# Even mixer of a two-block transformer: the scores of four forgetting heads in one TensorE group instead of two

## Chip, cores, metric

The kernel runs on one core of a Trainium2 chip. The metric is the device time of one execution in microseconds (us); a kernel's time is the median of its runs.

## What is computed

Two transformer blocks with 256 rows of 1024 columns run one after the other, each two layers deep. The change lies in the second block, in the even mixer of its first layer, which holds eight forgetting heads of width 64 beside four differential heads:

```python
def forgetting_attention(q, k, v, cum_logf):
    ...
    for qs in range(0, seq, Q_BLOCK):
        qe = qs + Q_BLOCK
        s = jnp.einsum('bqhd,bkhd->bhqk', q[:, qs:qe], k[:, :qe], preferred_element_type=jnp.float32) * scale
        s = s + cum_logf[:, :, qs:qe, None] - cum_logf[:, :, None, :qe]
        causal = jnp.arange(qs, qe)[:, None] >= jnp.arange(qe)[None, :]
        p = jax.nn.softmax(jnp.where(causal, s, -jnp.inf), axis=-1).astype(v.dtype)
        outs.append(jnp.einsum('bhqk,bkhd->bqhd', p, v[:, :qe]))
    return jnp.concatenate(outs, axis=1)

def even_mixer(h, w_in, ...):
    a_q, a_k, a_v, a_f, b_q, b_k, b_v = split_cols(h @ w_in, EVEN_SIZES)
    aq = rms_norm(a_q.reshape(bsz, seq, A_HEADS, HEAD_DIM), qk_gains[0])
    ak = rms_norm(a_k.reshape(bsz, seq, A_HEADS, HEAD_DIM), qk_gains[1])
    ...
    a_out = forgetting_attention(aq, ak, av, cum_logf).reshape(bsz, seq, A_WIDTH)
    ...
    b_out = differential_attention(bq, bk, bv, lam)
    b_out = (rms_norm(b_out, subln_gain) * (1.0 - lambda_init)).reshape(bsz, seq, B_WIDTH)
    return jnp.concatenate([a_out, b_out], axis=-1) @ w_out
```

After the mixer comes attention to a memory of 256 rows, whose keys and values (`mem_n @ w_kv`) do not depend on the mixer.

## The kernel before

**Large matmuls.** All weights stream from HBM. A unit of weights is 1024 columns wide in SBUF. ScalarE rounds it to `WH` (L1358), VectorE takes the rest as `WL` (L1647), and TensorE multiplies three times: `WH` and `WL` by the high part of the rows, `WH` by their low part (L1081, L1082, L1083). The three passes for 128 rows of the contraction and one of the two row tiles are called a step of large matmuls. Five units of `WH` and `WL` are held; ScalarE converts the next when TensorE has used up the oldest (`w_used`). A projection of 512 columns (a chunk) fills two of four large banks of PSUM, M0 and M1 or M2 and M3, one for each row tile.

**Small steps between them.** Four other banks, AUX0 to AUX3, serve all small products: turns (transposes of results that become rows for the next projection), scores, transposes of probabilities, products with the values. A small step takes the bank that the planner expects to be free first. TensorE waits at it until the bank's last user has been read out (`aux_out`).

**A forgetting head** goes through these steps. The scores of two heads (64 rows each, in the two halves of TensorE's rows) are one step on TensorE: L1242 and L1244 for the even head, L1243 and L1245 for the odd one, each head into its own AUX bank. VectorE adds the decay and the causal mask and takes the row maximum (L1929, L1930). ScalarE takes the exponentials with their sums into a buffer TMP, and with that the bank is free (L1563, L1564). VectorE divides by the sums (L1956 to L1961). TensorE transposes the three blocks of 128x128 (L1252) into another AUX bank, and ScalarE copies them to `PT` (L1585). After four heads TensorE multiplies them by the values (L1279, L1281), and ScalarE and VectorE take the high and low part of the result (L1529, L1703).

**The neighbours.** Around these steps the stage ends the differential heads: their outputs (L1263 to L1265) and two turns of their normalised result `BO` (L1124), read out by ScalarE (L1421) and VectorE (L1680). The large matmuls that run meanwhile are the memory's keys (`MTh`, `MTl`), two chunks, then the mixer's output projection (`XA0h`, `XA0l`). ScalarE evicts each chunk of keys with the sums of squares of its heads (L1401, L1405), and VectorE reduces them (L1865).

**The order.** `Plan` builds every step with a place `at`, counted in contraction steps of a 512-column chunk, one for both row tiles. TensorE takes the steps in the order of `at`. ScalarE and VectorE each take them in the order of `at` plus the step's own `late` plus a constant for the step's kind:

```python
act, dve = (sorted(steps, key=lambda s: (s.at + s.late + LATER.get(s.kind, (0.0, 0.0))[i], s.rank, s.seq)) for i in range(2))
```

For scores that constant is 2.2 on ScalarE and 0.9 on VectorE. The places of the forgetting heads come from the table `PLACES`: in `heads`, the scores of heads 2p and 2p+1 stand at `at + hg_s[p]`, where `at` is the end of the chunk of values; `hg_late[p]` is added for the odd head; normalisation, transposes and the products with the values stand at `hg_p`, `hg_pt` and `hg_o` behind the place of their own pair. Within an engine nothing is reordered at run time.

Of the kernel before, what the change touches and what calls it, by code (L numbers as in the profile page):

```python
# [32 lines left out]
    "df_late": (1.5, 0.6, -0.6, -0.1), "df_p": (3.1, 3.4, 3.4, 3.4), "df_pt": (5.9, 6.8, 6.2, 6.8), "df_o": (7.4, 9, 10.5, 8.3),  # L33
    "bo": (28, 28.5, 29.2, 30.1, 34.4, 36.7), "hg_s": (1.3, 6.6, 11.6, 16.3), "hg_late": (1.3, 1.3, 1.9, 2.5),
    "hg_p": (3, 5.4, 4.2, 5.4, 4.2, 5.4, 4.2, 6.6), "hg_pt": (5.6, 6.8, 5.6, 6.2, 5, 7.4, 6.5, 7.4), "hg_o": (7.6, 8.2),
    "od_s": (0.9, 6, 9.8, 15.5), "od_late": (0, 1.3, -1.2, 1.3), "od_p": (3, 5.4, 4.2, 4.2, 1.7, 5.4, 4.8, 6),
    "od_pt": (5.6, 9.3, 5.3, 7.5, 5.3, 6.5, 6.5, 7.7), "od_o": (9.6, 11.9), "odd": (25.7, 17.5, 0, 14.2, 0, 14.8, -7.2),
# [2366 lines left out]
```

## Time and profile before

| | us |
|---|---|
| median of 3 runs | 1864.65 (1864.58 to 1866.2) |
| profiled execution | 1865.1 |
| its span | 1862.7 |
| TensorE busy in the span | 1857.9 |
| VectorE, ScalarE busy | 1310.3, 1119.3 |
| the changed stage in the span | about 1018 to 1063 |

Times in the rows below are microseconds from the start of the span. TensorE is called PE there, its weight loads PEld, VectorE DVE, ScalarE ACT, GpSimd POOL and SyncE SP. In the chain of work a row's time is the step by which the end of the work moves on; in the timeline it is the instruction's own duration, which overlaps the next.

### The profile page before, as it was taken

Reading aid. Unit: us, or ns where it says so; the run is one execution under the profiler, and the core shown is the slowest. Engines: PE = TensorE matmul, PEld = TensorE weight load, DVE = VectorE, ACT = ScalarE, POOL = GpSimd, SP = SyncE. Lnnn points to the kernel's source line nnn. Section 1 sums busy time; section 2 is a strip of 40 time slices with the busy share of each in tenths; the row PEclk is TensorE's granted clock in tenths of the full one; section 3 lists DMA queues with packets and bytes.
Section 4 is the critical chain, followed back from the end, with each engine's and each line's share of the span. In section 5 each row is a group of like instructions: output and inputs, shape, how many; then the busy total and the mean of one; then the engine's idle time right before and its main releaser. Section 6 shows DMA issues by size and latency. Waiting matters only on the chain.

```text
span 1862.7 us, 25413 instructions
## 1 busy us (share of the span) xinstructions
PE 1857.9 (100%) x9293; PEld 1623.7 (87%) x9293; DVE 1310.3 (70%) x1949; ACT 1119.3 (60%) x1678; POOL 369.0 (20%) x606
## 2 busy tenths in 40 slices
PE   9999999999999999999999999999999999999999
PEld 8888988888889888888888889888888888899888
DVE  6776776667777776666577886776666578977664
ACT  6776655557766655555468785654555467765553
POOL 2101233111001431122103001531122111102320
PEclk9999999999999999999999999999999999999999
DMA  9767789878578997798765567997798788758984
GB/s 316 236 186 229 222 258 299 260 233 253 166 221 242 292 287 232 219 272 255 238 180 191 174 191 204 281 274 237 225 255 252 227 265 242 216 157 232 255 258 138
DMA packets 289803, 436.43 MB, mean 234 GB/s; under 512 B 25548, under 2 KB 170416, under 8 KB 289424
## 3 DMA queue, kind: packets, MB, share of 16 engines
q1 hardware_dynamic: 260384, 352.41, 61.9%
q0 software_dynamic: 28832, 82.07, 16.3%
q8 instruction: 74, 1.21, 0.3%
q14 instruction: 49, 0.40, 0.1%
q10 hardware_dynamic: 464, 0.34, 0.1%
HBM read 396.43 MB, written 38.29 MB: 233 GB/s over the span
## 4 chain that ended last, share of the span: by engine, by line
PE 99%; DMA 0%; DVE 0%; SPq 0%; ACT 0%; issue 0%; ACTq 0%
PE M L1081 31%; PE M L1083 31%; PE M L1082 31%; PE AUX L1124 1%; PE AUX L1138 0%; PE AUX L1252 0%; DMA RAW<-in_w_in 0%; PE AUX L1244 0%; PE AUX L1242 0%; PE AUX L1279 0%; PE AUX L1167 0%; PE AUX L1295 0%; PE AUX L1323 0%; PE AUX L1296 0%; PE AUX L1297 0%; PE AUX L1324 0%
## 5 line engine op out<-in xcount | busy, mean ns | idle before, releaser
L1647 DVE TENSOR_TENSOR WL<-RAW,WH 128x1024 fp32r<-128x1024 f32 (+1 forms) x669 | 810.8, 1217 | 383.5 <-ACT WH L1358 380.9
L1358 ACT ACTIVATE WH<-RAW 128x1024 fp32r<-128x1024 f32 (+1 forms) x670 | 705.0, 1055 | 518.8 <-PE M L1083 469.7
L1081 PE MATMUL M<-WH,Bh 128*128 128x512 f32 (+1 forms) x1820 | 691.3, 380 | 0.6 <-ACT TMP L1401 0.3
L1082 PE MATMUL M<-WL,Bh 128*128 128x512 f32 (+1 forms) x1820 | 683.1, 375 | 0.0
L1083 PE MATMUL M<-WH,Bl 128*128 128x512 f32 (+1 forms) x1820 | 683.1, 375 | 0.0
L1081 PEld LDWEIGHTS M<-WH,Bh 128*128 128x128 f32 x1820 | 344.2, 189 | 50.6 <-issue 4.2
L1083 PEld LDWEIGHTS M<-WH,Bl 128*128 128x128 f32 x1820 | 344.2, 189 | 47.1
L1082 PEld LDWEIGHTS M<-WL,Bh 128*128 128x128 f32 x1820 | 344.4, 189 | 44.7
L1396 ACT ACTIVATE AS<-M,KEEP 128x256 f32<-128x256 f32 x132 | 55.3, 470 | 80.3 <-PE M L1083 78.7
L1081 PE MATMUL M<-WH,MTh 128*128 128x512 f32 x128 | 51.0, 398 | 0.0
L1082 PE MATMUL M<-WL,MTh 128*128 128x512 f32 x128 | 48.5, 379 | 0.0
L1083 PE MATMUL M<-WH,MTl 128*128 128x512 f32 x128 | 48.5, 379 | 0.0
L2085 POOL DMA_DIRECT2D squares<-QT x4 | 3.0, 762 | 171.2 <-DVE QT L1772 171.2
L2098 POOL DMA_DIRECT2D HB0t<-squares x48 | 26.3, 555 | 50.0 <-DMA squares<-HB0b 45.7
L2098 POOL DMA_DIRECT2D HB1t<-squares x48 | 26.4, 556 | 47.0 <-DMA squares<-HB1b 30.0
L1745 DVE SCALAR_TENSOR_TENSOR X<-M,X 128x512 f32<-128x512 f32 (+1 forms) x54 | 30.5, 607 | 6.1 <-PE M L1083 6.1
L2098 POOL DMA_DIRECT2D HC0t<-squares x48 | 26.3, 554 | 43.1 <-DMA squares<-HC0b 42.2
L2078 POOL TENSOR_TENSOR KEEP<-SM,KEEP 128x2 f32<-128x2 f32 x15 | 13.3, 885 | 108.1 <-DVE SM L1723 98.6
L2098 POOL DMA_DIRECT2D HD0t<-squares x48 | 26.4, 557 | 41.2 <-DMA squares<-HD0b 41.1
L1082 PE MATMUL M<-WL,LA1h 128*128 128x512 f32 (+1 forms) x94 | 34.4, 366 | 0.0
L1083 PE MATMUL M<-WH,LA1l 128*128 128x512 f32 (+1 forms) x94 | 34.4, 366 | 0.0
L1081 PE MATMUL M<-WH,LA1h 128*128 128x512 f32 (+1 forms) x94 | 34.4, 366 | 0.0
(534 smaller groups left out, 2886.9 us busy)
## 6 DMA issues: line engine op xcount, KB each, us to landing
RAW<-in_ffn_w_in SPq DMA_DIRECT2D x352, 256.0 KB, 4.2
RAW<-in_w_in SPq DMA_DIRECT2D x103, 512.0 KB, 4.8
RAW<-in_w_gate_up SPq DMA_DIRECT2D x176, 256.0 KB, 4.4
RAW<-in_ffn_w_out SPq DMA_DIRECT2D x88, 512.0 KB, 4.6
RAW<-in_w_down SPq DMA_DIRECT2D x44, 512.0 KB, 4.9
RAW<-in_x_w_kv SPq DMA_DIRECT2D x32, 512.0 KB, 4.6
RAW<-in_even_w_in SPq DMA_DIRECT2D x24, 512.0 KB, 4.5
RAW<-in_odd_w_in SPq DMA_DIRECT2D x24, 512.0 KB, 5.4
```

The costliest lines, as they stand in the source:

```text
L1081: e.matmul(out, s.hi, wh, start=s.at0, stop=False)
L1082: e.matmul(out, s.hi, wl, start=False, stop=False)
L1083: i = e.matmul(out, s.lo, wh, start=False, stop=s.final)
L1124: tr = e.transpose(aux[:, i * P:(i + 1) * P], x, ident)
L1358: e.activation(hi, raw, ACT.Copy).then_inc(k.w_hi, 1)
L1396: e.activation(s.silu[t], banks[t][:, 0, :], ACT.Silu, scale=r[t]).then_inc(k.silu_made, 1)
L1647: e.tensor_tensor(lo, raw, hi.bitcast(F32), ALU.subtract).then_inc(k.w_lo, 1)
L1745: e.scalar_tensor_tensor(out=x, in0=banks[t], scalar=s.scale, in1=x, op0=ALU.mult, op1=ALU.add).then_inc(k.m_out[c.banks[t]], 1)
L2078: e.tensor_tensor(s.r, s.v, p.MHALF, ALU.pow).then_inc(k.r_made, 1)
L2085: e.dma_start(p.parked[x.slot, 0:4 * P * 32 * x.m].rearrange("(c p e) -> p c e", c=n, p=P), x.squares.rearrange("p (c e) -> p c e", c=n)). ...
L2098: e.dma_start(x.rows[32 * c:32 * c + 32, :].rearrange("p (q e) -> p q e", q=q), p.parked[x.slot, c * n:(c + 1) * n].rearrange("(q j e) -> ...
```

## The change

One row of numbers. The scores of heads 0 and 1 move from 1.3 to 6.6, where heads 2 and 3 stand; those of heads 4 and 5 move from 11.6 to 16.3, where heads 6 and 7 stand. The odd heads' delay on ScalarE and VectorE falls from 1.3 to 2.5 down to 0 for the first pair of a group and 0.6 for the second. Normalisations and transposes move with their scores, since they are placed relative to them; the products with the values stand where they did.

```diff
-    "bo": (28, 28.5, 29.2, 30.1, 34.4, 36.7), "hg_s": (1.3, 6.6, 11.6, 16.3), "hg_late": (1.3, 1.3, 1.9, 2.5),
+    "bo": (28, 28.5, 29.2, 30.1, 34.4, 36.7), "hg_s": (6.6, 6.6, 16.3, 16.3), "hg_late": (0, 0.6, 0, 0.6),
```

**TensorE, the first group of scores.** `KA` and `QA` are the heads' keys and queries, `M0` to `M3` the large banks, `CC` the identity for transposes. Before, heads 2 and 3 stand alone, with a transpose of head 0 behind them:

```order
L1083 MATMUL M1<-WH,MTl 128x512
L1242 MATMUL AUX1<-KA,QA 128x128
L1243 MATMUL AUX2<-KA,QA 128x128
L1244 MATMUL AUX1<-KA,QA 128x256
L1245 MATMUL AUX2<-KA,QA 128x256
L1252 MATMUL AUX3<-CC,TMP1 128x128 x3
L1081 MATMUL M0<-WH,MTh 128x512
```

With the change:

```order
L1083 MATMUL M1<-WH,MTl 128x512
L1242 MATMUL AUX0<-KA,QA 128x128
L1243 MATMUL AUX2<-KA,QA 128x128
L1244 MATMUL AUX0<-KA,QA 128x256
L1245 MATMUL AUX2<-KA,QA 128x256
L1242 MATMUL AUX1<-KA,QA 128x128
L1243 MATMUL AUX3<-KA,QA 128x128
L1244 MATMUL AUX1<-KA,QA 128x256
L1245 MATMUL AUX3<-KA,QA 128x256
L1081 MATMUL M0<-WH,MTh 128x512
```

Heads 0 and 1 came some ten steps earlier and now stand in the same group: four heads hold all four AUX banks.

**ScalarE, the exponentials behind the first chunk of keys.** Before (the exponentials of heads 0 and 1 stand further up, outside this piece):

```order
L1585 ACTIVATE PT0<-AUX0 128x384
L1401 ACTIVATE TMP1<-M0,KEEP 128x512
L1405 ACTIVATE AS<-TMP1 128x512
L1401 ACTIVATE TMP4<-M1,KEEP 128x512
L1405 ACTIVATE AS<-TMP4 128x512
L1563 ACTIVATE TMP0,SM<-AUX1,SM 128x128
L1564 ACTIVATE TMP0,SM<-AUX1,SM 128x256
L1358 ACTIVATE WH<-RAW 128x1024
L1563 ACTIVATE TMP3,SM<-AUX2,SM 128x128
L1564 ACTIVATE TMP3,SM<-AUX2,SM 128x256
L1421 ACTIVATE XA0h<-AUX3 128x512
```

With the change (behind the last row follow a conversion L1358, the turn's L1421 from AUX0, another L1358 and the copies L1585):

```order
L1401 ACTIVATE TMP4<-M0,KEEP 128x512
L1405 ACTIVATE AS<-TMP4 128x512
L1401 ACTIVATE TMP5<-M1,KEEP 128x512
L1405 ACTIVATE AS<-TMP5 128x512
L1563 ACTIVATE TMP0,SM<-AUX0,SM 128x128
L1564 ACTIVATE TMP0,SM<-AUX0,SM 128x256
L1563 ACTIVATE TMP1,SM<-AUX2,SM 128x128
L1564 ACTIVATE TMP1,SM<-AUX2,SM 128x256
L1563 ACTIVATE TMP2,SM<-AUX1,SM 128x128
L1564 ACTIVATE TMP2,SM<-AUX1,SM 128x256
L1563 ACTIVATE TMP3,SM<-AUX3,SM 128x128
L1564 ACTIVATE TMP3,SM<-AUX3,SM 128x256
```

All four heads' exponentials now stand behind the eviction of the chunk of keys in M0 and M1, heads 0 to 3 in TMP0 to TMP3. On TensorE the first turn, which wrote AUX3 before, now writes AUX0.

**TensorE's transposes and VectorE's normalisations of the first group, with the change.** TensorE, from the first transposes on (the first turn, L1124 into AUX0, stands four steps of large matmuls ahead):

```order
L1252 MATMUL AUX1<-CC,TMP0 128x128 x3
L1252 MATMUL AUX2<-CC,TMP2 128x128 x3
L1081 MATMUL M3<-WH,MTh 128x512
L1082 MATMUL M3<-WL,MTh 128x512
L1083 MATMUL M3<-WH,MTl 128x512
L1124 MATMUL AUX3<-CC,BO 128x128 x4
L1252 MATMUL AUX0<-CC,TMP3 128x128 x3
```

VectorE, from head 2's normalisation on:

```order
L1956 RECIPROCAL SM<-SM 128x2
L1960 TENSOR_SCALAR TMP2<-TMP2,SM 128x128
L1961 TENSOR_SCALAR TMP2<-TMP2,SM 128x256
L1647 TENSOR_TENSOR WL<-RAW,WH 128x1024
L1680 TENSOR_TENSOR XA0l<-AUX0,XA0h 128x512
L1956 RECIPROCAL SM<-SM 128x2
L1960 TENSOR_SCALAR TMP1<-TMP1,SM 128x128
L1961 TENSOR_SCALAR TMP1<-TMP1,SM 128x256
L1956 RECIPROCAL SM<-SM 128x2
L1960 TENSOR_SCALAR TMP3<-TMP3,SM 128x128
L1961 TENSOR_SCALAR TMP3<-TMP3,SM 128x256
```

Head 0 is normalised before this piece, then head 2, and heads 1 and 3 only after a weight conversion and the turn's low part. TensorE transposes heads 0, 2, 3 and 1 in this order; before, the four transposes lay between the large matmuls one by one.

## Rows read from the trace of the kernel before

**Rows 1.** The page: span, engines' busy time, granted clock in 40 slices

```profile
span 1862.7 us, 25413 instructions
PE 1857.9 (100%) x9293; PEld 1623.7 (87%) x9293; DVE 1310.3 (70%) x1949; ACT 1119.3 (60%) x1678; POOL 369.0 (20%) x606
...
PEclk9999999999999999999999999999999999999999
```

**Rows 2.** TensorE's waits over the span: us in total, times, longest us

```profile
PE M L1031 <- DVE WARM L1621: 1.1, 1, 1.1
...
PE M L1081 <- ACT TMP L1401: 0.3, 1, 0.3
```

**Rows 3.** The chain of work, 1030 to 1042: start us, us, what

```profile
1030.94 0.48 PE AUX L1252 x3
...
1037.37 0.22 PE M L1081
1037.58 0.22 PE M L1082
1037.80 0.21 PE M L1083
...
1038.66 0.30 PE AUX L1242
...
1038.97 0.10 PE AUX L1242
...
1039.52 0.41 PE M L1081
...
1040.36 0.33 PE AUX L1252 x3
...
1041.34 0.44 PE AUX L1124 x4
```

**Rows 4.** ScalarE's timeline, 1032 to 1038: start us, us, instruction [idle before <-releaser]

```profile
1032.81 1.06 ACT L1358 ACTIVATE WH<-RAW 128x1024 fp32r<-128x1024 f32 x1 [0.87 <-PE M L1083]
1033.78 0.48 ACT L1585 ACTIVATE PT<-AUX 128x384 f32<-128x384 f32 x1
1034.14 0.68 ACT L1401 ACTIVATE TMP<-M,KEEP 128x512 f32<-128x512 f32 x1
...
1036.63 0.35 ACT L1563 ACTIVATE TMP<-AUX,SM 128x128 f32<-128x128 f32 x1
...
1037.42 1.05 ACT L1358 ACTIVATE WH<-RAW 128x1024 fp32r<-128x1024 f32 x1
```

**Rows 5.** TensorE's timeline: the first matmul of the second chunk of keys

```profile
1032.55 0.38 PE L1081 MATMUL M<-WH,MTh 128*128 128x512 f32 x1
```

**Rows 6.** VectorE's timeline, 1033 to 1041

```profile
1033.57 0.30 DVE L1929 CUSTOM_DVE_ANT_0 AUX<-AUX,NB 128x128 f32<-128x128 f32 x1
...
1034.79 1.23 DVE L1647 TENSOR_TENSOR WL<-RAW,WH 128x1024 fp32r<-128x1024 f32 x1
1035.93 1.52 DVE L1865 TENSOR_REDUCE SM<-AS 128x2 f32<-128x512 f32 x2
...
1037.56 0.17 DVE L1956 RECIPROCAL SM<-SM 128x2 f32<-128x2 f32 x1
...
1037.96 0.35 DVE L1961 TENSOR_SCALAR TMP<-TMP,SM 128x256 f32<-128x256 f32 x1
1038.51 1.23 DVE L1647 TENSOR_TENSOR WL<-RAW,WH 128x1024 fp32r<-128x1024 f32 x1 [0.19 <-ACT WH L1358]
1039.80 0.69 DVE L1680 TENSOR_TENSOR XA0l<-AUX,XA0h 128x512 fp32r<-128x512 f32 x1
1040.40 0.15 DVE L1956 RECIPROCAL SM<-SM 128x2 f32<-128x2 f32 x1
```

**Rows 7.** ScalarE's copy of the eighth head, and the product with the values that waits for it

```profile
1060.41 0.49 ACT L1585 ACTIVATE PT<-AUX 128x384 f32<-128x384 f32 x1 [1.14 <-PE AUX L1252]
...
1061.04 0.65 PE L1279 MATMUL AUX<-PT,VA 128*64 128x256 f32 x4
```

## Prediction

> **What bounds the kernel now.** Read the page first: TensorE is busy for the whole span and its granted clock stands at full speed in every slice [rows 1]. Then TensorE's waits: the longest after the opening is 0.3 us, and nothing near the changed place is in the list [rows 2]. So the order of TensorE's queue is the time: whatever is taken out of that queue is gained in full, and whatever makes it stand is lost in full, because no wait later on is long enough to take it back. The third view is the chain of work through the forgetting heads [rows 3]. It shows at what intervals TensorE ends its work, and so what a group of scores costs beyond its own columns. The last is the timelines of ScalarE and VectorE there [rows 4, 6]: both have work in hand and small gaps, and they follow TensorE. What matters is how far behind it they are when TensorE needs one of their results.
>
> **What the change takes out.** The scores of a pair of heads are eight short passes. A pair standing alone pays on the way in: its first pass takes 0.30 us, the same pass of the second half 0.10 us, so 0.20 us is extra. It pays on the way out: the large matmul behind it takes 0.41 us instead of 0.22, 0.19 us extra [rows 3]. One of the four pairs is followed by transposes, which take 0.48 instead of 0.33 us, 0.15 us extra [rows 3]. Before: 4 x 0.20 + 3 x 0.19 + 0.15 = 1.52 us. After: two groups of two pairs, 2 x (0.20 + 0.19) = 0.78 us. **Saving 0.74 us.** The trace has no two pairs back to back. Inside a pair the step from one head's half to the next costs nothing [rows 3], which is the nearest row, so I take the full saving; the other end is that the second pair pays as if it stood alone, a saving of nothing. Nothing else is removed: row maxima, exponentials, normalisations, transposes and copies are as many as before, no transfer is added, and the queues of POOL and SP are not touched.
>
> **What it adds: two waits behind the first group.** Write T for the moment when TensorE finishes the chunk of memory keys in banks M0 and M1. That chunk ends two steps of large matmuls after the group. Behind T TensorE's new order is: five steps of large matmuls (three passes of 0.22, 0.22 and 0.21 us, 0.65 us each [rows 3]), so 3.25 us, and then the first turn of the differential result, which now writes AUX0. AUX0 holds the scores of head 0 and comes free when ScalarE has taken head 0's exponentials. Before, this turn wrote AUX3, long free.
>
> ScalarE's new order puts all four heads' exponentials behind the eviction of that same chunk. From T, by its rows: the conversion of the next weights starts 0.26 us after the next chunk's first matmul (1032.81 against 1032.55 [rows 4, 5]); it is followed 0.97 us later; the eviction with its squares takes 1034.14 to 1036.63, 2.49 us; one head's exponentials take 1036.63 to 1037.42, 0.79 us [rows 4]. From the end of a ScalarE result to TensorE's start on it are 0.14 us (1060.90 to 1061.04 [rows 7]). Sum 0.26 + 0.97 + 2.49 + 0.79 + 0.14 = 4.65 us. **First wait 4.65 - 3.25 = 1.40 us.** Before, heads 0 and 1 had their exponentials ahead of this eviction, and nothing on TensorE hung on heads 2 and 3 so soon.
>
> The second wait is at the transposes of head 3, third of the four transposes in TensorE's new order. They need head 3's normalised rows, and VectorE normalises in the order 0, 2, 1, 3. It puts a weight conversion and the low part of the turn ahead of heads 1 and 3. That conversion needs the ScalarE conversion that now stands behind the four exponentials. From T: 0.26 + 0.97 + 2.49, four heads 4 x 0.79 = 3.16, the ScalarE conversion 1.05 [rows 4], hand-over 0.04 (1038.47 to 1038.51 [rows 4, 6]), VectorE's conversion 1.14 (1034.79 to 1035.93), the turn's low part 0.60 (1039.80 to 1040.40), two normalisations of 0.75 (1037.56 to the end of L1961 at 1038.31 [rows 6]) and 0.14 to TensorE: 11.35 us. TensorE's own work from T to there: nine steps of matmuls 5.85, two turns 0.88 (0.44 each), two heads' transposes 0.66, one more step 0.65: 8.04 us. **Both waits together 11.35 - 8.04 = 3.31 us**, of which 1.91 us is the second. What is queued behind TensorE in both waits is everything, since its queue is in order.
>
> The reductions of the squares (1.52 us at 1035.93 [rows 6]) stand ahead of head 2 on VectorE, but run under ScalarE's exponentials and conversion. The row maxima are not late: two heads take 1033.57 to 1034.79, 1.22 us, four 2.44 us [rows 6]; with a conversion of 1.14 us ahead they end about 2.3 us behind T, and ScalarE asks for the first at 0.26 + 0.97 + 2.49 = 3.72 us. All four banks are free when the group starts: the last user of AUX3, the differential output, is now 8 steps of matmuls, 5.2 us, ahead of it.
>
> Bounds of the 3.31 us: if heads 1 and 3 did not have to stand behind VectorE's conversion it would be 1.14 us less, 2.2 us; if ScalarE's conversion meets a weight buffer that TensorE, standing still, has not yet released, half a microsecond more, 3.8 us. I take 3.3, as each term has its row.
>
> **The second group** has ten steps of matmuls, 6.5 us, before its first transposes, and no turn writes one of its banks. But the transposes of its last two heads now stand back to back, one step of matmuls ahead of the product with the values; there the chain shows TensorE with hardly any slack now (the copy ends at 1060.90, the product starts at 1061.04 [rows 7]). I add 0.1 us, between 0 and 0.4.
>
> **Sum:** -0.74 + 3.31 + 0.10 = +2.67 us. The profiled execution took 1865.1 us (span 1862.7 us) and would become 1867.8; it is 0.45 us above the median of the three runs, 1864.65, so the forecast against that median is **1867.3 us**. With the bounds, +1.5 to +4.0: 1866.1 to 1868.7. About 0.2%, 3.7 us, is what a measurement of this kernel can tell from no change, so this is no measurable change, on the slow side.
>
> The rows say that a group over all four banks leaves the turn no free one. Of the Trainium skill, Perfetto Trace Analysis, section Matmuls, says that independent groups should rotate through the banks, so that one is evacuated under the next one's matmuls; that speaks against this change. By it alone the whole 4.65 us to the first free bank would be lost, 3.25 us more than here; the rows put five steps of matmuls over it, so I do not follow it that far.
>
> **The rivals.** (a) The banks come free in time: ScalarE reaches the exponentials earlier than its order lets me see, and the saving stands alone, -0.74 + 0.10: 1864.0 us. For it: ScalarE has gaps of up to 0.87 us there [rows 4]. Against: the gap ends with the release of the very chunk it must evict. Chance 0.10. (b) Only the first wait comes, VectorE being ahead: -0.74 + 0.10 + 1.40, 1865.4 us. Chance 0.10. (c) Slower: the second group stalls as the first does, at the transposes of its last head. By the same rows its last normalisation ends about 0.4 us before TensorE asks for it, so it decides if ScalarE, which evicts the next keys first, begins the exponentials 0.4 us later than I have it. The price is at most that of the second wait, 1.91 us: 1869.2 us. Chance 0.10. (d) The pairs do not share their way in and out: +0.74, 1868.0 us. Chance 0.03. (e) The clock falls. It is at full speed throughout, also around the 1.1 us wait at the start [rows 1, 2]; should it go to half from the first wait to the product with the values, some 5.2 us of work would take as much again: 1872.5 us. TensorE: Matmul & The Clock Gate of the Trainium skill (A second HAM failure mode) tells of such a fall where the engine idles often between groups as it cycles through banks. Two waits in one place are not often. Chance 0.03. The forecast keeps 0.64.
>
> **The numbers.** The range leaves out (a) and (e), 0.13, and takes in (b), (c) and (d): 1865.0 to 1869.3 us. Slower by over 0.2% means above 1868.4: (c), (e) and the upper end of the forecast, 0.14. Faster by over 0.2% needs 3.7 us, and there is no such amount to save: 0.02. No change by that measure: 0.84.
>
> **What would show it.** In the changed profile TensorE's waits should list the turn L1124 with about 1.4 us, waiting for ScalarE's L1564, and the transposes L1252 with about 1.9 us, waiting for VectorE's L1961; the chain should show 0.30 and 0.41 us at two groups instead of four. The first product with the values should come about 1.9 us later than before, the second 2.7 us. No wait at L1124 or L1252 would make me wrong, and so would a third one of over a microsecond in the second group.

## The result and the profile after

The changed kernel takes **1867.44 us** (median of 22 runs, 1866.91 to 1868.7). The kernel before, run beside it, takes 1865.01 us (22 runs, 1864.39 to 1867.08). The ratio is 1.0013 with a 95% interval of 1.0007 to 1.0019: slower by 2.4 us. The interval does not hold 1, so the loss is there, but it lies within the 0.2% that counts as no change here. The profiled execution took 1866.96 us, its span is 1865.2 us.

The page of the changed kernel, the lines that answer to [rows 1]:

```profile
span 1865.2 us, 25412 instructions
PE 1857.2 (100%) x9293; PEld 1623.9 (87%) x9293; DVE 1309.8 (70%) x1949; ACT 1119.1 (60%) x1678; POOL 369.4 (20%) x606
...
PEclk9999999999999999999999999999999999999999
```

The clock is still full in every slice, the same instructions run on TensorE, and its busy time is even 0.7 us less than in [rows 1]. The span is 2.5 us longer all the same, so TensorE must stand somewhere. TensorE's waits over the span of the changed kernel (us in total, times, longest us) say where:

```profile
PE AUX L1252 <- DVE TMP L1961: 1.5, 1, 1.5
PE AUX L1124 <- ACT TMP L1564: 1.3, 1, 1.3
```

Both lines are new against [rows 2], and no others of that size are. TensorE's timeline of the changed kernel shows where they stand, and that the group itself has become cheaper:

```profile
1028.95 0.37 PE L1242 MATMUL AUX<-KA,QA 64*128 64x128 f32 x1
...
1029.16 0.27 PE L1242 MATMUL AUX<-KA,QA 64*128 64x128 f32 x1
...
1029.70 0.27 PE L1242 MATMUL AUX<-KA,QA 64*128 64x128 f32 x1
1029.81 0.27 PE L1242 MATMUL AUX<-KA,QA 64*128 64x128 f32 x1
...
1036.60 0.63 PE L1124 MATMUL AUX<-CC,BO 128*128 128x128 f32 x4 [1.34 <-ACT TMP L1564]
...
1043.05 0.55 PE L1252 MATMUL AUX<-CC,TMP 128*128 128x128 f32 x3 [1.49 <-DVE TMP L1961]
...
1063.57 0.65 PE L1279 MATMUL AUX<-PT,VA 128*64 128x256 f32 x4
```

From the first pass to the second the first pair takes 0.21 us, the second pair 0.11 us: the second pair pays no way in. The first wait ends at the first turn, the second at the third of the four transposes. The first product with the values starts at 1045.80, 1.82 us later than in the kernel before (1043.98), the second at 1063.57, 2.53 us behind [rows 7].

The executions do not all begin the stage at the same moment: its first output of a differential head (L1263) starts between 1018.12 and 1019.08 us in the profiles below, for reasons further up in the span that are not followed here. So I compare kernels by **the distance** from that L1263 to the second product. It is 42.91 us before (1018.13 to 1061.04) and 45.45 us with the change (1018.12 to 1063.57): +2.54 us, all of the difference in the span.

The chain of work through the second wait, as the changed kernel's chain has it (start us, us, what):

```profile
1035.65 0.35 ACT TMP L1563 x2
...
1038.42 0.46 ACT TMP L1564 x2
1038.87 0.96 ACT WH L1358
1039.83 0.02 issue
1039.86 1.23 DVE WL L1647
1041.08 0.60 DVE XA0l L1680
...
1042.74 0.27 DVE TMP L1961
1043.01 0.04 issue
1043.05 0.55 PE AUX L1252 x3
```

It runs through four exponentials, one ScalarE conversion, one VectorE conversion, the turn's low part and two normalisations. That is the order that the prediction counted up.

### The profile page after: what moved, and what is told of

It reads as the page before. It is cut to its first block, busy times and chain, and to the rows that moved or that the text cites. A ratio compares the mean times of both kernels' runs of the same rounds, so it can differ in the third digit from the quotient of the medians.

```text
span 1865.2 us, 25412 instructions
## 1 busy us (share of the span) xinstructions
PE 1857.2 (100%) x9293; PEld 1623.9 (87%) x9293; DVE 1309.8 (70%) x1949; ACT 1119.1 (60%) x1678; POOL 369.4 (20%) x606
## 3 DMA queue, kind: packets, MB, share of 16 engines
q8 instruction: 74, 1.21, 0.3%
## 4 chain that ended last, share of the span: by engine, by line
PE 98%; ACT 0%; DVE 0%; DMA 0%; SPq 0%; issue 0%; ACTq 0%
PE M L1081 31%; PE M L1083 31%; PE M L1082 31%; PE AUX L1124 1%; PE AUX L1138 0%; PE AUX L1252 0%; DMA RAW<-in_w_in 0%; PE AUX L1244 0%; DVE WL L1647 0%; PE AUX L1242 0%; PE AUX L1279 0%; PE AUX L1167 0%; PE AUX L1295 0%; PE AUX L1323 0%; PE AUX L1297 0%
## 5 line engine op out<-in xcount | busy, mean ns | idle before, releaser
L1358 ACT ACTIVATE WH<-RAW 128x1024 fp32r<-128x1024 f32 (+1 forms) x670 | 704.7, 1055 | 518.2 <-PE M L1083 471.2
L2098 POOL DMA_DIRECT2D HC1t<-squares x48 | 26.3, 556 | 39.4 <-DMA squares<-HC1b 39.4
```

Of the source, the lines that this page charges most:

```text
L1358: e.activation(hi, raw, ACT.Copy).then_inc(k.w_hi, 1)
L2098: e.dma_start(x.rows[32 * c:32 * c + 32, :].rearrange("p (q e) -> p q e", q=q), p.parked[x.slot, c * n:(c + 1) * n].rearrange("(q j e) -> ...
```

## The experiments

The theory: what costs time is the order on ScalarE and VectorE, and the bank that the turn holds; the group of four itself is cheaper. The rival: four heads at once are a longer chain, and cost it wherever their steps stand. Each experiment is judged by the distance against the kernel before (+2.54 us is the change's), taken from one profiled execution of each kernel; the edit of experiment 2, profiled again as experiment 8, gave the same distance to 0.01 us. Every diff below is against the changed kernel.

| experiment | TensorE's waits in the stage, us, in order | distance against before, us | runs | time, us |
|---|---|---|---|---|
| the change | L1124 1.34, L1252 1.49 | +2.54 | 22 | 1867.44 |
| 1 first group only | L1124 1.35, L1252 0.62 and 1.23 | +3.64 | 1 | 1868.1 |
| 2, 8 second group only | L1252 0.48; 0.48 | +0.36; +0.35 | 1; 11 | 1866.33; 1865.65 |
| 3 normalisations ahead | L1124 1.35, L1252 1.21 | +2.25 | 1 | 1866.93 |
| 4, 9 turns later | L1252 1.17 and 1.91; 1.16 and 1.91 | +4.44; +4.21 | 1; 10 | 1869.12; 1869.11 |
| 5 exponentials ahead | L1252 1.26 and 1.42 | +2.42 | 1 | 1866.97 |
| 7 exponentials and normalisations ahead | L1252 1.44 | +0.93 | 1 | 1865.58 |
| 6 all three | none | -0.46 | 11 | 1864.48 |

### 1. Only the first group

```diff
-    "hg_s": (6.6, 6.6, 16.3, 16.3), "hg_late": (0, 0.6, 0, 0.6),
+    "hg_s": (6.6, 6.6, 11.6, 16.3), "hg_late": (0, 0.6, 1.9, 2.5),
```

> Only heads 0 to 3 stand in one group; heads 4 to 7 as before. If the loss lies behind the first group (theory): TensorE still waits about 1.3 us at L1124 and 1.5 us at L1252, and the second product with the values starts at about 1063.9 (1063.57 with the change, plus 0.37 for the way in and out that the second group no longer shares, less up to 0.1). If it lay in holding four banks as such, half of it would go: waits of about 1.4 us in all, about 1062.4.

1868.1 us. TensorE's waits in this kernel:

```profile
PE AUX L1252 <- DVE XA0l L1680: 1.9, 2, 1.2
PE AUX L1124 <- ACT TMP L1564: 1.4, 1, 1.4
```

The wait for the exponentials is the change's. Behind it the transposes wait twice, and for L1680, VectorE's low part of a turn: here they go to a bank that a turn still holds. With heads 4 and 5 left at 11.6, their scores stand on TensorE between these steps, hold two of the four banks, and take one more way in and out. So the first group is what costs, and half of the change costs 1.10 us more (3.64 - 2.54) than all of it. The theory had the first wait right. The second it had as one of 1.5 us, where two came, 1.85 us together and for L1680, and the second product came at 1064.69 instead of 1063.9. The rival's 1.4 us of waits in all does not hold either. Of the 1.10 us, 0.37 is listed waiting (3.20 against 2.83) and 0.37 is what the expectation reckons for the way in and out; the rest is not accounted for.

### 2 and 8. Only the second group

```diff
-    "hg_s": (6.6, 6.6, 16.3, 16.3), "hg_late": (0, 0.6, 0, 0.6),
+    "hg_s": (1.3, 6.6, 16.3, 16.3), "hg_late": (1.3, 1.3, 0, 0.6),
```

> Only heads 4 to 7 stand in one group. Theory: no wait of TensorE above 0.3 us beside those of the kernel before; the second product with the values at about 1060.8 (1061.04 before, less 0.37 for one way in and out, plus 0.1). If a group of four costs by itself (rival), a wait of 1 us or more at its transposes and about 1062.

1866.33 us, but this execution began the stage at 1019.06 us, 0.93 us late. By the distance the edit costs 0.36 us, where the theory had a gain of 0.24 us (1060.8 against 1061.04) and no wait over 0.3 us: a miss. A wait of 0.48 us came. It was therefore run again with more runs:

> Only heads 2 and 3 moved to the later place (three groups of TensorE in the layer instead of four or two), as in the first look at this edit, with more runs, to see whether the 0.93 us that the profile was late ahead of the place, and the 0.5 us wait for L1961, come again. Theory (half the change has half the saving and a small wait): second product 0 to 0.5 us later than in the kernel before, reckoned from the first L1263 of the layer, median within 0.6 us of before, ratio 0.9998 to 1.0003. Rival (any group moved costs the whole chain): second product 2 us later, ratio 1.0010 or more.

(The heads that this edit moves are 4 and 5; the text on record misnames them.) Median 1865.65 us against 1865.05, ratio 1.0003 (0.9994 to 1.0012). This profile began only 0.26 us late, and its distance is +0.35 us. The wait came again, in TensorE's timeline:

```profile
1041.46 0.55 PE L1252 MATMUL AUX<-CC,TMP 128*128 128x128 f32 x3 [0.48 <-DVE TMP L1961]
```

The wait is not in the second group. It stands at head 3's transposes in the first, where the scores of heads 4 and 5 stood before (1038.66 to 1039.52 in [rows 3]). Taking them away took cover from VectorE's normalisation: VectorE ends it 23.02 us behind the first L1263 in this kernel (1041.41) as in the kernel before (1041.15), but TensorE is there 0.9 us earlier. The small price, which the second expectation had, holds; the rival's 2 us does not.

### 3. The normalisations ahead of the reductions and the conversion

```diff
-    "hg_p": (3, 5.4, 4.2, 5.4, 4.2, 5.4, 4.2, 6.6),
+    "hg_p": (3.2, 3.3, 3.4, 3.5, 4.2, 5.4, 4.2, 6.6),
```

> VectorE normalises heads 0, 1, 2 ahead of the reductions of the squares and head 3 right behind them, all ahead of the weight conversion. If the second wait comes from heads 1 and 3 standing behind the conversion (as the prediction had it in its lower bound), it shrinks by about 1.1 us: L1252 waits 0.4 us, second product at about 1062.4. If VectorE's whole work on that stretch sets it (rival), the bank AUX0 stays shut by the turn's low part L1680 instead, only VectorE's idle 0.57 us goes, L1252 waits about 0.9 us for L1680, and the product starts at about 1063.0. The first wait stays at 1.3 us by both.

1866.93 us, distance +2.25. Head 3's normalised rows are there at 1041.16, but TensorE starts its transposes at 1043.03. TensorE's and VectorE's timelines of this kernel:

```profile
1043.03 0.52 PE L1252 MATMUL AUX<-CC,TMP 128*128 128x128 f32 x3 [1.21 <-DVE XA0l L1680]
```

```profile
1040.81 0.35 DVE L1961 TENSOR_SCALAR TMP<-TMP,SM 128x256 f32<-128x256 f32 x1
1041.07 1.22 DVE L1647 TENSOR_TENSOR WL<-RAW,WH 128x1024 fp32r<-128x1024 f32 x1
1042.20 0.68 DVE L1680 TENSOR_TENSOR XA0l<-AUX,XA0h 128x512 fp32r<-128x512 f32 x1
```

The wait shrank by 0.28 us, not by the 1.14 us of the conversion, and has another releaser. So the theory's 0.4 us fails; the rival named the right releaser, but had 0.9 us for the 1.21. Head 3's transposes go to AUX0, where the first turn stands until L1680 has read it, and L1680 stands behind the same conversion. The second wait has two holders, one behind the other.

### 4 and 9. The turns behind head 3's transposes

```diff
-    "bo": (28, 28.5, 29.2, 30.1, 34.4, 36.7),
+    "bo": (28, 28.5, 29.2, 30.1, 37.2, 38.3),
```

> Both turns of the differential result move behind the transposes of head 3, so that no turn writes a bank of the group before its exponentials. If the two waits are two causes (rival), the 1.3 us at L1124 go and the rest stays: second product at about 1062.1. If one chain from the chunk's end over ScalarE and VectorE to head 3 sets the sum (theory), the waits move to the transposes L1252 of heads 2 and 3 and still come to about 3.4 us: second product at 1063.6 to 1063.9.

1869.12 us, distance +4.44. No wait is left at L1124; the transposes wait 1.17 and 1.91 us, 3.08 together instead of 2.83. Taking the first wait away gains nothing, since the same chain on ScalarE and VectorE is met one step later. So the rival fails, and the theory's waits came, 0.3 us short of the 3.4 expected, but the second product came at 1065.72 instead of 1063.6 to 1063.9. Some 1.6 us of the +4.44 are not in the waits, and the windows of this kernel show what they are (us, busy of PE, PEld, DVE, ACT, POOL, then the granted clock, the DMA share and GB/s):

```profile
1042.00:1043.00 1.00, 0.30 (x2) 0.30 (x3) 0.96 (x4) 0.00 (x0) 0.00 (x0) 0.90 0.13 43
1043.00:1044.00 1.00, 1.00 (x5) 0.91 (x4) 0.78 (x1) 0.41 (x1) 0.00 (x0) 0.50 0.94 346
1044.00:1045.00 1.00, 1.00 (x4) 0.71 (x4) 0.00 (x0) 0.08 (x1) 0.00 (x0) 0.50 0.47 166
1045.00:1046.00 1.00, 1.00 (x8) 1.00 (x6) 0.00 (x0) 0.00 (x0) 0.00 (x0) 0.50 0.68 203
1046.00:1047.00 1.00, 1.00 (x6) 0.92 (x5) 0.00 (x0) 0.63 (x2) 0.00 (x0) 0.89 0.78 299
```

The clock falls to half at the end of the second wait. To see whether that belongs to the order or to the one execution, it was run again:

> The change with TensorE's turns for the norm behind head 3's transposes, as in the first look at this edit, to see whether the granted clock falls again behind the two waits that stand close together. Theory (the order of the waits makes the clock fall): a stretch of two us behind the second wait again with a granted clock of 0.5 to 0.7, and 1868.5 to 1869.5 us, ratio 1.0018 to 1.0026. Rival (chance of that one execution): granted clock 1.00 in every stretch, 1866.5 to 1867.5 us, ratio 1.0008 to 1.0015.

1869.11 us (10 runs), ratio 1.0021 (1.0012 to 1.003), as the theory had it. The fall came again, at the same place in the order, this time within the wait, which ends at 1043.41:

```profile
1042.00:1043.00 1.00, 0.00 (x0) 0.00 (x0) 0.93 (x6) 0.48 (x2) 0.00 (x0) 0.99 0.00 0
1043.00:1044.00 1.00, 0.59 (x4) 0.60 (x4) 1.00 (x3) 0.00 (x0) 0.00 (x0) 0.50 0.75 90
```

It did not come every time. In 7 of the 10 runs the mean clock of the span was 0.999, and their median is 1869.59 us; in three it was 1.000, and these are the three fastest, 1867.25 to 1867.98 us, where the rival had 1866.5 to 1867.5. TensorE's timeline gives the price. The eight starts from these transposes to the second large matmul behind the next ones

```profile
1043.41 0.90 PE L1252 MATMUL AUX<-CC,TMP 128*128 128x128 f32 x3 [1.91 <-DVE TMP L1961]
...
1046.86 0.38 PE L1082 MATMUL M<-WL,MTh 128*128 128x512 f32 x1
```

take 3.45 us (1043.41 to 1046.86). The steps between them at full clock are 0.30 + 0.30 + 0.22 + 0.22 + 0.43 + 0.25 + 0.30 = 2.02 us, the first four from other places of this kernel, the last three from the kernel before, where a turn and transposes follow each other too. The fall costs 1.43 us here, and by the same reckoning 1.67 us in the first execution (1042.70 to 1046.39, 3.69 us). With it the distances add up: the change's, the longer waits and the fall are 2.54 + 0.25 + 1.67 = 4.46 us in experiment 4 (measured 4.44) and 2.54 + 0.24 + 1.43 = 4.21 us in experiment 9 (measured 4.21).

### 5. The exponentials ahead of the eviction of the keys

```diff
-                s.late = PLACES[f"{which}_late"][hp] * hh
+                s.late = PLACES[f"{which}_late"][hp] * hh - (1.2 if which == "hg" and hp < 2 else 0)
```

> All four heads' scores at the later place as in the change, but the exponentials and row maxima of heads 0 to 3 are put ahead of the evictions of the four chunks on ScalarE and VectorE. Theory (VectorE runs its instructions in order, and the reductions of the chunks' squares, now waiting for the later evictions, and the squares' conversion still stand between the four normalisations): the wait at L1124 goes, L1252 waits 1.6 to 2.0 for head 2 and 1.4 to 1.7 for head 3, 3.0 to 3.7 together, and the second product with values comes 2.2 to 3.0 us later than in the kernel before, no earlier than in the change. Rival (the eviction ahead of the exponentials alone makes the wait): both waits go, the second product comes 0.5 to 0.8 us earlier than before.

The term counts on both engines, so VectorE's row maxima move up with the exponentials. 1866.97 us, distance +2.42. TensorE's waits:

```profile
PE AUX L1252 <- DVE TMP L1961: 2.7, 2, 1.4
```

The wait at L1124 is gone, as both expected. The exponentials of head 3 end at 1035.84 instead of 1038.88, three microseconds earlier, and the kernel gains 0.12 us: the normalisations of heads 2, 1 and 3 still stand on VectorE behind the reductions of the squares, which end 0.6 us later than in the change (1039.05 against 1038.43), and those of heads 1 and 3 behind the conversion and L1680 as well. The theory gave 3.0 to 3.7 us for the two waits, and no gain on the change; it is 2.68, a little less, with that gain of 0.12. The rival, that the exponentials alone make the wait, falls.

### 7. Exponentials and normalisations ahead, the turns left

This is experiment 5 with 1.4 for 1.2, and with the first four numbers of `hg_p` at (1.3, 1.4, 1.5, 1.6).

> All four heads' scores at the later place; exponentials and normalisations of heads 0 to 3 ahead of the evictions and the reductions, as in the experiment with three edits, but TensorE's turns for the norm left where the change has them, so that the second turn's bank is held until VectorE's low parts of it (L1680), which stand behind the reductions and a conversion. Theory (the bank is a wait of its own): no wait at L1124, and L1252 ahead of the first product waits 0.7 to 1.4 for L1680; second product with values 0.3 to 1.0 us later than in the kernel before, reckoned from the first L1263 of the layer. Rival (with exponentials and normalisations early the bank does not matter): no wait over 0.3 us, second product 0.4 to 0.7 us earlier than before.

1865.58 us, distance +0.93. One wait is left, in TensorE's timeline, and VectorE's timeline (first the end of head 3's normalisation) shows that head 3 had been ready for 4.4 us:

```profile
1041.67 0.52 PE L1252 MATMUL AUX<-CC,TMP 128*128 128x128 f32 x3 [1.44 <-DVE XA0l L1680]
```

```profile
1036.92 0.35 DVE L1961 TENSOR_SCALAR TMP<-TMP,SM 128x256 f32<-128x256 f32 x1
...
1040.84 0.68 DVE L1680 TENSOR_TENSOR XA0l<-AUX,XA0h 128x512 fp32r<-128x512 f32 x1
```

So the bank is a holder by itself, worth 1.44 us, a touch more than the 0.7 to 1.4 expected.

### 6. All three

Experiment 7 with the turns at 37.2 and 38.3, as in experiment 4.

> All four heads' scores at the later place as in the change, with exponentials and all four normalisations ahead of the evictions and the reductions on their engines, and TensorE's turns for the norm behind the transposes of head 3. Theory (order on ScalarE, VectorE and the bank held by the turn together make the wait; the group itself is cheaper): no wait over 0.5 us at L1124 or L1252 before the first product, second product 0.4 to 0.8 us earlier than in the kernel before, 1864.2 to 1864.6 us, ratio 0.9995 to 0.9998. Rival (one group of four heads costs in itself, by its longer chain of four row maxima and exponentials ahead of any product): waits of 1 us or more stay at the transposes of heads 2 and 3, second product 0.5 to 2 us later than before, 1865.5 to 1867 us.

Median 1864.48 us (11 runs) against 1865.10 (15 runs), ratio 0.9998 (0.9989 to 1.0007). TensorE's waits over the whole span:

```profile
PE M L1031 <- DVE WARM L1621: 1.1, 1, 1.1
PE M L1081 <- ACT TMP L1401: 0.3, 1, 0.3
PE M L1081 <- DVE Bl L1674: 0.2, 1, 0.2
```

None is left in the stage, and the distance is 42.45 us, 0.46 less than before, near the low end of what the theory expected. The rival falls: four heads at once cost nothing when the work that follows them is not late and no turn holds their bank. Of the 0.74 us that the prediction had as saving, 0.27 is lost in one step of TensorE:

```profile
1040.30 0.60 PE L1124 MATMUL AUX<-CC,BO 128*128 128x128 f32 x4
1041.00 0.52 PE L1252 MATMUL AUX<-CC,TMP 128*128 128x128 f32 x3
```

From the turn to the transposes are 0.70 us, against 0.43 in the kernel before. What holds them is not in the list of waits, but ScalarE's timeline has a likely holder, the first of four copies of transposes:

```profile
1040.39 1.66 ACT L1585 ACTIVATE PT<-AUX 128x384 f32<-128x384 f32 x4
```

By the plan of this kernel these transposes, head 1's, write AUX0, which head 0's hold until that first copy. The copies take 0.48 us each, so it ends at 1040.87, 0.13 us ahead of the transposes, about the hand-over of 0.14 in [rows 7]. No experiment moved the copy. The kernel beats the change (1867.44). Against the kernel before it is 0.6 us lower by the medians, and its interval holds 1, so a gain over that one is not shown by the times.

## Why the prediction was right

Forecast 1867.3 us, measured 1867.44; forecast +2.67 us, measured +2.43 by the medians and +2.54 by the distance. Point by point, each by the steps from one start on TensorE to the next in the two timelines:

- **What bounds it.** The order of TensorE's queue is the time: the spans of the profiled executions follow their distances to within 0.3 us (leaving aside experiments 2 and 9, which began 0.9 us late), so no wait was made up for later.
- **The saving, forecast 0.74 us.** All steps but those at the turns and products came out 0.65 us shorter. The groups themselves give the whole 0.74, since the chain of the changed kernel has the way in, 0.30 us, only at 1029.02 and 1050.11 and the way out, 0.41 us, only at 1030.53 and 1051.62; the first steps behind the two waits are 0.08 us longer together (0.38 for 0.35 and 0.30 for 0.25). The second pair of a group shares the way in and out, so rival (d) falls.
- **The first wait, forecast 1.40 us.** The profile lists 1.34. The step from the last large matmul to the turn, with that of the second turn, grew from 0.44 to 1.93 us, 1.49 us. T, the end of the chunk in M0 and M1, is 1031.86 and the turn starts at 1036.60: 4.74 us, against 4.65 added up from rows.
- **The second wait, forecast 1.91 us.** Listed 1.49; the step from the turn to the transposes grew from 0.43 to 2.09 us, 1.66 us. From T to its end are 11.19 us, forecast 11.35. Both together 3.15 us, forecast 3.31: the term was 0.16 us too large. ScalarE's and VectorE's other steps came out within 0.04 us of their rows; the excess lies in the two normalisations (1.40 us, counted as 1.50) and the hand-over to TensorE (0.05, counted as 0.14). Experiments 5 and 7 show its parts, ScalarE's order, VectorE's order and the bank.
- **The second group, forecast 0.10 us.** The steps ahead of the two products grew by 0.05 us. There is no wait there, so rival (c) falls.
- **The sum.** -0.65 + 3.15 + 0.05 = +2.55 us. These are a split of the measured distance, so the sum itself checks nothing; what bears the forecast out is that each of its three terms came out within 0.16 us. That the medians agree to 0.2 us is in part luck, since the runs of one kernel differ by 1.8 us and more.
- **What was wrong.** The lower bound said that heads 1 and 3 without VectorE's conversion ahead of them would wait "1.14 us less". Experiment 3 made just that, and gained 0.28: the bank under the turn was a second holder that the bound left out. For these transposes the chain counted only what they read, not where they write.
- **Rivals (a), (b) and (e).** Both waits came, so (a) and (b) fall. The clock of (e) stayed at full speed in the change, but (e) is no empty fear: experiments 4 and 9 show it, with two waits not much longer than the change's. The prediction gave it 0.03, on the ground that two waits in one place are not often. In those kernels two waits were enough, in 8 of 11 runs.

The Trainium skill's advice that the prediction weighed (Perfetto Trace Analysis, section Matmuls: independent groups rotate through the banks) points the right way in experiments 3 and 7, where the bank alone held TensorE for 1.21 and 1.44 us. The cost is what the bank is held beyond the cover, as the rows said, and not the whole of its use.

## What to carry to other kernels

When steps are gathered into one group to save TensorE's way in and out, their followers on the other engines have to be moved with them: here the saving was 0.7 us and the followers, left in their old order, cost 3.15. Before moving a step, list for its first user on TensorE all that it needs, both the data that it reads and the bank that it writes, and what stands ahead of each on the other engines. If several holders end at about the same time, taking one away shows little: here one alone brought 0.1 or 0.3 us, two together 1.6, all three 3.0.

## What had not been expected of the hardware

The granted clock can fall at two short waits. In experiments 4 and 9 TensorE stood for 1.17 and 1.16 us, worked for 1.2 us, and stood for 1.91 us. The clock fell to 0.50, the lower level of 1.2 GHz, at about 1042.8 in experiment 4, just behind that wait, and at about 1043.0 in experiment 9, 0.4 us before it ended, and stayed there for 3.4 us in each (in experiment 9 the windows from 1042 on have 0.99, 0.50, 0.50, 0.50 and 0.80). With 1.26 us, then 1.6 us of work, then 1.42 us (experiment 5) the clock stayed at 1.00, as the window of its second wait and the one behind it show:

```profile
1042.00:1043.00 1.00, 0.00 (x1) 0.00 (x1) 0.96 (x6) 0.00 (x0) 0.00 (x0) 1.00 0.52 104
1043.00:1044.00 1.00, 1.00 (x6) 0.91 (x7) 1.00 (x1) 0.42 (x2) 0.00 (x0) 1.00 0.92 356
```

It stayed at 1.00 in the change too, with 1.34 and 1.49 us and 5.0 us of work between, and in experiment 1, whose three waits come to 3.20 us. An order with 0.4 us more waiting than that of experiment 5 (3.08 against 2.68) lost a further 1.4 to 1.7 us through the clock where it fell. Three of the ten runs of experiment 9 have a mean clock of 1.000 in the same order; what decides it is not shown.
